# An expert layer by gathered rows, and by dense matmuls over both whole tables

## The chip, the cores and the metric

The kernel runs on one core of one Trainium2 chip. The metric is the device time of a launch in microseconds (us), lower is better; all data are float32. Engines: PE (TensorE, matmuls; PEld its weight loads), DVE (VectorE), ACT (ScalarE), POOL (GpSimd), SP (SyncE, which issues DMAs).

## What is computed

Two transformer blocks on 256 tokens of width 2048. The first mixes four kinds of token mixer and a convolutional FFN of width 5632, the second has a sparse and a sliding-window attention and then a layer of 16384 experts, which is what the change touches:

```python
def peer(xn, wq, subkeys, u, v):
    q = (xt @ wq).reshape(T, PEER_HEADS, 2, PEER_QDIM // 2)
    s1 = jnp.einsum('thd,nd->thn', q[:, :, 0], subkeys[0])
    s2 = jnp.einsum('thd,nd->thn', q[:, :, 1], subkeys[1])
    v1, i1 = lax.top_k(s1, PEER_TOPK)
    v2, i2 = lax.top_k(s2, PEER_TOPK)
    cand = (v1[..., :, None] + v2[..., None, :]).reshape(T, PEER_HEADS, -1)
    sc, ci = lax.top_k(cand, PEER_TOPK)
    idx = e1 * PEER_NKEYS + e2        # e1, e2: i1, i2 at ci // 16, ci % 16
    gate = jax.nn.softmax(sc, axis=-1)
    h = jax.nn.gelu(jnp.einsum('cd,chkd->chk', xc, u[idx]))
    return jnp.einsum('chk,chkd->cd', gate * h, v[idx])
```

There are 8 heads with 16 picks each, so 128 picks a token. An expert's number is a row e1 and a column e2 of a grid of 128 x 128. The tables u and v have 16384 rows of 2048 floats, 134 MB each. After the layer come the residual sum, a last norm and the output.

## The kernel before

Tokens stand in two tiles of 128 (t = 0, 1), one token a partition; `x` holds the residual stream [128, 2, 2048], and `hT` the normed input turned, [128 features, 16, 256 tokens]. Weights are streamed by SP in units of 1 MB through `ring`, four slots of 8 KB a partition: a unit is loaded when the matmuls on the slot's earlier unit have counted `unit_used`, and PE waits on the slot's semaphore. `project` (L789) multiplies on 512 columns, the FFN's up and gate projections (L1041) on 256, its down projection (L1054) on 512 with whole 8 KB rows in the ring.

The expert layer of before follows out2, the second block's output projection:

- `norm(4)`, `norm_turn(3)` (L773) and `norm_cols(3)` (L488) make hT. PE then makes the queries with each token tile by itself (L1189): eight blocks of 128 matmuls on 128 columns, each followed by ACT's copy out of PSUM (L727), which PE waits for. Keys are scored (L1198) and copied by ACT (L730), eight banks in all.
- DVE picks: the best 16 of 128 on 16 sides (`choose_sides`, L1699 to L1706), the best 16 of 256 sums in 8 heads (`choose_sums`), the experts' numbers (`name_experts`, L1739 to L1746), the softmax (`pick_weights`, L1753 to L1759) with ACT's exp (L734) between. For tile 1 this is cut up among the first steps of tile 0.
- POOL copies eight expert numbers (L447) and starts eight indirect DMAs (L456): each brings one row of u for each of 128 tokens, 1 MB, into one of eight row slots (four in `proj`, four in `ring`). Over both tiles and both tables that is 512 gathers.
- DVE takes each gathered row: a product with the token's input summed to one number (L1773, 256 times) for u, and after ACT's gelu of all of them, x += weight * row (L1811, 256 times) for v. Every use returns the slot to POOL by `row_used`.

```python
slot = row_slots[s % ROWS]
link(vec.tensor_tensor_reduce(slot, slot, xs[:, t], 1.0, 0.0, ALU.mult, ALU.add, peer["h16"][:, 0, s:s + 1]), "row_used", wait=(s == 15))
```

The end is L1814 (x is complete), the norm, the scaling by final_norm (L1818) and two stores by SP.

Of the kernel before, what the change touches and what calls it, by code (L numbers as in the profile page):

```python
# [156 lines left out]
def build(nc, a, out, scratch):  # L171
# [120 lines left out]
    choice = [carve(base, {"hot": (PICKS, TOP), "val": (SIDES, TOP), "at_f": (SIDES, TOP), "hi_f": (1, PICKS), "lo_f": (1, PICKS), "e1": (1, PICKS), "e2": (1, PICKS)})
              for base in (flat_proj, arena[:])]
    spare = flat_proj[:, 4 * D:]
    peer |= carve(spare, {"best": (2 * HEADS, TOP), "h": (2, PICKS), "weight": (2, PICKS), "keys": (2, P), "keysT": (2, P), "h16": (1, 16), "total": (1, 2 * HEADS),
                          "at_u": (2 * SIDES, TOP), "pick_u": (2 * HEADS, TOP), "expert": (2, PICKS), "now": (2, 8)})
    row_slots = [flat_proj[:, D * s:D * (s + 1)] for s in range(4)] + [ring[:, s].rearrange("p k n -> p (k n)") for s in range(4)]
# [1550 lines left out]
```

## Time and profile before

| | us |
|---|---|
| median of 3 runs | 3982.63 |
| lowest, highest | 3982.62, 3986.85 |
| span of the profiled execution | 3985.6 |
| PE busy / DVE busy in it | 2187.0 / 1962.2 |
| ACT busy / POOL busy in it | 343.6 / 1297.3 |
| moved by DMA | 932.83 MB |

The page lists the profiled execution by its span, first to last instruction, and gives no other time of it; the three runs' times lie between 3.0 us below that span and 1.3 above it. A line such as L1773 is a line of the kernel; a group shows its name and shapes, how often it ran, its busy time and mean ns, and how long its engine was idle ahead of it and on whom. The clock column is the granted TensorE clock as a share of full speed.

### The profile page before, as it was taken

Reading aid. Unit: us, or ns where it says so; the run is one execution under the profiler, and the core shown is the slowest. Engines: PE = TensorE matmul, PEld = TensorE weight load, DVE = VectorE, ACT = ScalarE, POOL = GpSimd, SP = SyncE. Lnnn points to the kernel's source line nnn. Section 1 sums busy time; section 2 is a strip of 40 time slices with the busy share of each in tenths; the row PEclk is TensorE's granted clock in tenths of the full one; section 3 lists DMA queues with packets and bytes.
Section 4 is the critical chain, followed back from the end, with each engine's and each line's share of the span. In section 5 each row is a group of like instructions: output and inputs, shape, how many; then the busy total and the mean of one; then the engine's idle time right before and its main releaser. Section 6 shows DMA issues by size and latency. Waiting matters only on the chain.

```text
span 3985.6 us, 26773 instructions
## 1 busy us (share of the span) xinstructions
PE 2187.0 (55%) x8774; PEld 1503.0 (38%) x8774; DVE 1962.2 (49%) x2297; ACT 343.6 (9%) x713; POOL 1297.3 (33%) x712
## 2 busy tenths in 40 slices
PE   0899853588999999998898898700000000000000
PEld 0444642545888887443448756700000000000000
DVE  7664165311000000001004511799998888888887
ACT  0000222101011110000103501000000000000000
POOL 2111140000000000000000000177788888888886
PEclk9999875789999999999997999955555555555555
DMA  9898200023444444443640035799899999999998
GB/s 375 333 416 349 67 34 0 1 86 136 157 148 152 153 148 147 157 148 115 203 144 18 0 110 187 282 403 411 341 416 391 374 390 372 374 373 376 378 359 340
DMA packets 236362, 932.83 MB, mean 234 GB/s; under 512 B 20059, under 2 KB 25363, under 8 KB 164115
## 3 DMA queue, kind: packets, MB, share of 16 engines
q0 software_dynamic: 99840, 637.57, 40.1%
q1 hardware_dynamic: 136197, 294.46, 21.7%
q8 instruction: 28, 0.46, 0.0%
q14 instruction: 25, 0.20, 0.0%
q10 hardware_dynamic: 272, 0.13, 0.0%
HBM read 928.91 MB, written 2.15 MB: 234 GB/s over the span
## 4 chain that ended last, share of the span: by engine, by line
PE 50%; DVE 22%; DMA 10%; POOL 8%; issue 6%; ACT 2%; DVEq 0%; SPq 0%; POOLq 0%; ACTq 0%
PE ps L789 16%; PE ps L1041 15%; PE ps L1054 8%; DVE x L1811 6%; POOL ring L456 4%; DVE ring L1773 4%; DVE proj L1773 4%; PE ps L1189 3%; POOL proj L456 3%; DMA ring<-in_w_in 3%; DMA proj<-in_peer_v,proj 2%; DMA ring<-in_peer_u,proj 2%; DMA ring<-in_peer_v,proj 2%; DMA arena<-in_w_mod 1%; DVE arena L1261 1%
## 5 line engine op out<-in xcount | busy, mean ns | idle before, releaser
L447 POOL COPY proj<-proj 128x8 int32 x64 | 109.8, 1716 | 1999.7 <-DVE proj L1746 1957.0
L1041 PE MATMUL ps<-hT,ring 128*128 128x256 f32 x2816 | 608.0, 379 | 1.4 <-ACT hT L488 1.4
L1041 PEld LDWEIGHTS ps<-hT,ring 128*128 128x128 f32 x2816 | 535.0, 190 | 74.3 <-issue 1.7
L789 PE MATMUL ps<-ring,hT 128*128 128x512 f32 (+2 forms) x1216 | 492.8, 567 | 12.1 <-DMA ring<-in_w_in 10.7
L1811 DVE SCALAR_TENSOR_TENSOR x<-proj,x 128x2048 f32<-128x2048 f32 x128 | 301.3, 2354 | 84.2 <-DMA proj<-in_peer_v,proj 73.7
L789 PEld LDWEIGHTS ps<-ring,hT 128*128 128x128 f32 x1216 | 226.1, 197 | 279.0 <-issue 255.4
L1811 DVE SCALAR_TENSOR_TENSOR x<-ring,proj,x 128x2048 f32<-128x2048 f32 x128 | 301.0, 2352 | 30.2 <-DMA ring<-in_peer_v,proj 13.4
L1054 PE MATMUL ps<-ring,arena 128*128 128x512 f32 x704 | 304.1, 595 | 2.7 <-ACT arena L651 2.7
L456 POOL DMA_INDIRECT ring<-in_peer_v,proj x128 | 291.9, 2281 | 39.0 <-issue 39.0
L1773 DVE CUSTOM_DVE_ANT_0 proj<-proj,yT 128x2048 f32<-128x2048 f32 x128 | 288.5, 2289 | 21.4 <-DMA proj<-in_peer_u,proj 18.2
L1773 DVE CUSTOM_DVE_ANT_0 ring<-ring,yT 128x2048 f32<-128x2048 f32 x128 | 289.5, 2292 | 18.6 <-DMA ring<-in_peer_u,proj 17.5
L456 POOL DMA_INDIRECT proj<-in_peer_v,proj x128 | 267.4, 2089 | 58.6 <-issue 29.3
L456 POOL DMA_INDIRECT proj<-in_peer_u,proj x128 | 257.2, 2009 | 57.9 <-issue 29.3
L456 POOL DMA_INDIRECT ring<-in_peer_u,proj x128 | 237.6, 1856 | 40.4 <-issue 38.7
L789 PE MATMUL ps<-ring,yT 128*128 128x512 f32 x512 | 223.0, 598 | 13.6 <-DVE yT L1414 12.6
L1054 PEld LDWEIGHTS ps<-ring,arena 128*128 128x128 f32 x704 | 134.3, 191 | 172.1 <-issue 172.1
L1560 DVE SCALAR_TENSOR_TENSOR arena<-ps,vcols,arena 128x255 f32<-128x255 f32 x44 | 18.2, 476 | 331.0 <-ACT arena L644 331.0
L1261 DVE SCALAR_TENSOR_TENSOR arena<-arena,c_col 128x1024 f32 x120 | 154.2, 1285 | 49.9 <-DMA arena<-in_w_mod 46.8
L397 POOL DMA_DIRECT2D arena<-in_w_mod x96 | 67.8, 706 | 287.3 <-DVE arena L1261 178.7
L1575 DVE TENSOR_TENSOR arena<-ps,gates 128x512 f32<-128x512 f32 x8 | 5.2, 686 | 305.5 <-PE ps L1054 305.4
L789 PEld LDWEIGHTS ps<-ring,yT 128*128 128x128 f32 x512 | 98.2, 192 | 138.5 <-issue 138.5
L1569 DVE TENSOR_TENSOR proj<-arena,ps 128x1024 f32 x11 | 13.4, 1221 | 227.4 <-PE ps L1041 227.4
(379 smaller groups left out, 2250.8 us busy)
## 6 DMA issues: line engine op xcount, KB each, us to landing
arena<-in_w_mod POOLq DMA_DIRECT2D x96, 1024.0 KB
ring<-in_w_in SPq DMA_DIRECT2D x68, 1024.0 KB, 12.8
ring<-in_ffn_w_gate SPq DMA_DIRECT2D x44, 1024.0 KB, 5.1
ring<-in_ffn_w_up SPq DMA_DIRECT2D x44, 1024.0 KB, 5.2
ring<-in_ffn_w_down SPq DMA_DIRECT2D x44, 1024.0 KB, 4.8
ring<-in_w_out SPq DMA_DIRECT2D x32, 1024.0 KB, 5.1
ring<-in_peer_wq SPq DMA_DIRECT2D x32, 1024.0 KB, 5.0
arena<-bias_rows SPq DMA_DIRECT2D x1, 4096.0 KB, 14.4
```

Source lines behind the costliest of these rows:

```text
L397: pool_eng.dma_start(mod["ring"][:, j % 4], w_mod[:, 2 * j:2 * j + 2, cols]).then_inc(sem(f"mod_slot{j % 4}"), 16)
L447: pool_eng.tensor_copy(expert_now[:, half, :], expert[:, t, bass.ds(i * (2 * ROWS) + ROWS * half, ROWS)]).then_inc(sem("experts_now"), 1)
L456: pool_eng.indirect_dma_start(row_slots[s], None, table, bass.IndirectOffsetOnAxis(expert_now[:, half, s:s + 1], 0))\
L789: ins = pe.matmul(ps[:, 2 * (b % 2) + t, 0:w], lhs[:, KS * s + k, P * t:P * (t + 1)], ring[:, s, k, 0:w], start=(s == 0 and k == 0), stop= ...
L1041: ins = pe.matmul(ps[:, 4 * m + f, 0:T], ring[:, s, k, P * f:P * (f + 1)], hT[:, KS * s + k, :], start=(s == 0 and k == 0), stop=(s == SLO ...
L1054: ins = pe.matmul(ps[:, 2 * n + t, :], ffn["act"][:, par, s, P * t:P * (t + 1)], ring[:, s, n, :], start=(start and s == 0), stop=(stop an ...
L1189: ins = pe.matmul(ps[:, f, 0:P], ring[:, s, k, P * f:P * (f + 1)], hT[:, KS * s + k, P * t:P * (t + 1)], start=(s == 0 and k == 0), stop=( ...
L1261: ins = vec.scalar_tensor_tensor(out=to, in0=w, scalar=c, in1=to, op0=ALU.mult, op1=ALU.add)
L1560: ins = vec.scalar_tensor_tensor(out=ffn["gate"][:, f, 1:T], in0=ps[:, f, 0:T - 1], scalar=vcols[:, 1, bass.ds(i * 4 + (44 + f), 1)], in1= ...
L1569: link(vec.tensor_tensor(act_store[:, bass.ds(i * 4, 4), :], ffn["gate"], ps[:, 4:8, 0:T], ALU.mult), "up_free", wait=False)
L1773: link(vec.tensor_tensor_reduce(slot, slot, xs[:, t], 1.0, 0.0, ALU.mult, ALU.add, peer["h16"][:, 0, s:s + 1]), "row_used", wait=(s == 15))
L1811: link(vec.scalar_tensor_tensor(out=x[:, t], in0=row_slots[s % ROWS], scalar=peer["weight"][:, t, bass.ds(i * 16 + s, 1)], in1=x[:, t], op ...
```

## The change

Both tables are read whole, once, in order. Experts with the same column e2 form block b = e2 of 128 experts (partition e1); the host lays u out as [block, feature in a group of 128, group, expert] and v as [block, expert, feature], so that a block is 1 MB and 8 KB a partition in both.

- SBUF: yT, gates, proj and arena become parts of one tensor `big`, whose 128 KB a partition later hold `G` [expert row, block, token].
- Queries for both token tiles together: four blocks of 64 matmuls on 256 columns, in PSUM banks 0 to 3 and 4 to 7 in turn. Scores of both tiles follow, 64 matmuls.
- Hidden layer for every expert: block b is 16 matmuls of 128 x 128 by 256 tokens in bank b % 4, and ACT's gelu of them. For blocks 0 to 39 it goes to G[:, b]; meanwhile DVE picks for both tiles, then exp and softmax.
- The picks (row, column, weight) are turned by PE. For each token, 128 picks by 128 rows one-hot times the weight, and 128 picks by 128 columns one-hot, are made by DVE, four tokens a group; their product on PE is the dense 128 x 128 matrix of weights of that token. In group s (of 64) DVE multiplies the columns of blocks below 40 + s into G, ACT copies the others into G, and block 40 + s is computed in between; `weigh` later multiplies a block's gelu, left in PSUM, into G for the tokens already there.
- Table v: block b is 8 matmuls of G[:, b] by 512 features, all 8 PSUM banks accumulate over 128 blocks, and two DVE operations add them to x.
- Gathers, POOL's part in the layer, L1773 and L1811 are gone. Constants shrink and load in two tables, ffn_norm no longer as rows, final_norm at the end into hT.

```diff
-for _n, _c in (("in1", 12), ("out1", 4), ("up", 22), ("down", 11), ("in2", 7), ("out2", 4), ("wq", 8)):
+for _n, _c in (("in1", 12), ("out1", 4), ("up", 22), ("down", 11), ("in2", 7), ("out2", 4), ("wq", 4), ("u", 32), ("v", 32)):
...
-    yT = sb("yT", [P, KT, T])
+    flat_hT = hT[:].rearrange("p k t -> p (k t)")
+    big = sb("big", [P, P * T])
+    yT = big[:, 0:2 * D].rearrange("p (k t) -> p k t", t=T)
+    gates = big[:, 2 * D:4 * D].rearrange("p (g n) -> p g n", g=2)
+    proj = big[:, 4 * D:4 * D + NT * W1].rearrange("p (t n) -> p t n", t=NT)
+    arena = big[:, 4 * D + NT * W1:4 * D + NT * W1 + 12800]
...
+    G = big[:].rearrange("p (b t) -> p b t", t=T)
+    GROUP = 4
+    GROUPS = T // GROUP
+    FIRST = 40
+    hot = carve(tab[:, TAB_AT["anti"][0]:], {"row": (2, GROUP, P), "col": (2, GROUP, P)})
+    row_of = vrows[:].rearrange("p a b -> p (a b)")[:, 0:T]
+    col_of = vrows[:].rearrange("p a b -> p (a b)")[:, T:2 * T]
+    weight_of = vcols[:].rearrange("p a b -> p (a b)")[:, 0:T]
...
+        stream(w1v["peer_wq_2"], BLK["wq"], 4, 0)
+        load("norm_in", flat_hT[:, 0:D], a["final_norm_2"].partition_broadcast(P))
...
+        for name, table in (("u", a["peer_u_2"]), ("v", a["peer_v_2"])):
+            with sp.Fori(0, P // SLOTS) as i:
+                for s in range(SLOTS):
+                    sp.wait_ge(*at("unit_used", i * SLOTS + (BLK[name] * SLOTS + s - SLOTS + 1)))
+                    sp.dma_start(ring[:, s].rearrange("p k n -> p (k n)").unsqueeze(1), table.rearrange("b p n -> p b n")[:, bass.ds(i * SLOTS + s, 1), :])\
+                      .then_inc(sem(f"slot{s}"), 16)
...
-        for phase, table in enumerate((a["peer_u_2"], a["peer_v_2"])):
-            for t in range(NT):
-                pool_eng.wait_ge(*at("experts", t + 1))
-                base = PICKS * (NT * phase + t)
-                with pool_eng.Fori(0, PICKS // (2 * ROWS)) as i:
-                    for half in range(2):
...
-                        pool_eng.tensor_copy(expert_now[:, half, :], expert[:, t, bass.ds(i * (2 * ROWS) + ROWS * half, ROWS)]).then_inc(sem("experts_now"), 1)
-                        for s in range(ROWS):
...
-                            pool_eng.sem_inc(sem("pool_turn"), 1)
-                            pool_eng.indirect_dma_start(row_slots[s], None, table, bass.IndirectOffsetOnAxis(expert_now[:, half, s:s + 1], 0))\
-                                    .then_inc(sem(f"row{s}"), 16)
...
+        def hidden(b, i, bank):
+            act.wait_ge(*at("unit_used", i + (SLOTS * BLK["u"] + b + 1)))
+            to = G[:, b, :] if isinstance(i, int) else G[:, bass.ds(i + b, 1), :].rearrange("p o t -> p (o t)")
+            act.activation(to, ps[:, bank, 0:T], ACT.Gelu_apprx_tanh).then_inc(sem("hidden"), 1)
...
+        with act.Fori(0, 20, SLOTS) as i:
+            for s in range(SLOTS):
+                hidden(s, i, s)
+        best_exp(0)
+        with act.Fori(20, 36, SLOTS) as i:
+            for s in range(SLOTS):
+                hidden(s, i, s)
+        best_exp(1)
+        for b in range(36, FIRST):
+            hidden(b, 0, b % 4)
+        for s in range(GROUPS):
+            b = FIRST + s
+            n = GROUP * (s + 1)
+            act.wait_ge(*at("unit_used", SLOTS * BLK["u"] + b + 1))
+            if n < T:
+                act.activation(G[:, b, n:T], ps[:, b % 4, n:T], ACT.Gelu_apprx_tanh)
+            act.activation(ps[:, b % 4, 0:n], ps[:, b % 4, 0:n], ACT.Gelu_apprx_tanh).then_inc(sem("hidden"), 1)
+            act.wait_ge(*at("spread_vec", s + 1))
+            act.copy(G[:, b:P, GROUP * s:GROUP * (s + 1)], ps[:, 4 + s % 2, :].rearrange("p (t e) -> p e t", t=GROUP)[:, b:P, :]).then_inc(sem("spread_act"), 1)
+        for b in range(FIRST + GROUPS, P):
+            act.wait_ge(*at("unit_used", SLOTS * BLK["u"] + b + 1))
+            act.activation(ps[:, b % 4, 0:T], ps[:, b % 4, 0:T], ACT.Gelu_apprx_tanh).then_inc(sem("hidden"), 1)
...
+        def wq_block(i, par):
+            for s in range(SLOTS):
+                pe.wait_ge(sem(f"slot{s}"), i * 32 + 16 * (BLK["wq"] + par + 1))
+                for k in range(KS):
+                    for f in range(4):
+                        ins = pe.matmul(ps[:, 4 * par + f, 0:T], ring[:, s, k, P * f:P * (f + 1)], hT[:, KS * s + k, :],
+                                        start=(s == 0 and k == 0), stop=(s == SLOTS - 1 and k == KS - 1))
+                ins.then_inc(sem("unit_used"), 1)
...
+        wq_block(0, 0)
+        pe.wait_ge(*at("keys_out", 1))
+        wq_block(0, 1)
+        for par in range(2):
+            pe.wait_ge(*at("wq_out", par + 1))
+            wq_block(1, par)
+        pe.wait_ge(*at("wq_out", 4))
...
+        def hidden(i, b):
+            s = b % SLOTS
+            pe.wait_ge(sem(f"slot{s}"), i * (16 // SLOTS) + 16 * (BLK["u"] + b // SLOTS + 1))
+            rows = ring[:, s].rearrange("p k n -> p (k n)")
+            for k in range(KT):
+                ins = pe.matmul(ps[:, b % 4, 0:T], rows[:, P * k:P * (k + 1)], hT[:, k, :], start=(k == 0), stop=(k == KT - 1))
+            ins.then_inc(sem("unit_used"), 1)
...
+        for b in range(4):
+            pe.wait_ge(*at("score_out", b + 1))
+            hidden(0, b)
+        with pe.Fori(0, 32, SLOTS) as i:
+            for s in range(SLOTS):
+                pe.wait_ge(*at("hidden", i + (s + 1)))
+                hidden(i, 4 + s)
+        pe.wait_ge(*at("score_out", 8))
+        pe.wait_ge(*at("picked", NT))
+        for m in range(3):
+            for t in range(NT):
+                q = NT * m + t
+                ins = pe.transpose(ps[:, 6 + q // 4, P * (q % 4):P * (q % 4 + 1)], peer["pick"][:, m, t, :], ident)
+        ins.then_inc(sem("picks_turned"), 1)
+        for b in range(36, FIRST):
+            pe.wait_ge(*at("hidden", b - 3))
+            hidden(0, b)
+        for s in range(GROUPS):
+            b = FIRST + s
+            pe.wait_ge(*at("hot", s + 1))
+            if s >= 2:
+                pe.wait_ge(*at("spread_act", s - 1))
+                pe.wait_ge(*at("spread_vec", s - 1))
+            for j in range(GROUP):
+                ins = pe.matmul(ps[:, 4 + s % 2, P * j:P * (j + 1)], hot["row"][:, s % 2, j, :], hot["col"][:, s % 2, j, :],
+                                start=True, stop=True)
+            ins.then_inc(sem("spread"), 1)
+            pe.wait_ge(*at("hidden", b - 3))
+            if s >= 4:
+                pe.wait_ge(*at("weighed", s - 3))
+            hidden(0, b)
+        for b in range(FIRST + GROUPS, P):
+            pe.wait_ge(*at("weighed", b - FIRST - 3))
+            hidden(0, b)
+        pe.wait_ge(*at("weighed", P - FIRST))
+        pe.wait_ge(*at("spread_vec", GROUPS))
+        for b in range(P):
+            s = b % SLOTS
+            pe.wait_ge(*at(f"slot{s}", 16 * (BLK["v"] + b // SLOTS + 1)))
+            for t in range(NT):
+                for n in range(4):
+                    ins = pe.matmul(ps[:, 4 * t + n, :], G[:, b, P * t:P * (t + 1)], ring[:, s, n, :], start=(b == 0), stop=(b == P - 1))
+            ins.then_inc(sem("unit_used"), 1)
...
-        def dot_rows(i, t):
-            for s in range(16):
-                arrived(i, PICKS * t, s)
-                slot = row_slots[s % ROWS]
-                link(vec.tensor_tensor_reduce(slot, slot, xs[:, t], 1.0, 0.0, ALU.mult, ALU.add, peer["h16"][:, 0, s:s + 1]), "row_used", wait=(s == 15))
-            link(vec.tensor_copy(peer["h"][:, t, bass.ds(i * 16, 16)], peer["h16"][:, 0, :]))
...
+            vec.wait_ge(*at("score_out", 4 * t + 4))
+            choose_sides(t, range(SIDES))
+            add_sides(t)
+            choose_sums(t, range(HEADS))
+            shift_best(t)
+            name_experts(t)
+        for t in range(NT):
+            pick_weights(t)
+        vec.wait_ge(*at("picks_turned", 1))
+        vec.tensor_copy(row_of, ps[:, 6, 0:T])
+        vec.tensor_copy(col_of, ps[:, 6, T:2 * T])
+        link(vec.tensor_copy(weight_of, ps[:, 7, 0:T]))
+        def one_hot(s):
+            if s >= 2:
+                vec.wait_ge(*at("spread", s - 1))
+            for j in range(GROUP):
+                t = GROUP * s + j
+                vec.tensor_scalar(hot["row"][:, s % 2, j, :], tb("iota"), row_of[:, t:t + 1], weight_of[:, t:t + 1], ALU.is_equal, ALU.mult)
+            wide = [P, GROUP, P]
+            vec.tensor_tensor(hot["col"][:, s % 2], tb("iota").unsqueeze(1).to_broadcast(wide), col_of[:, GROUP * s:GROUP * (s + 1)].unsqueeze(2).to_broadcast(wide), ALU.is_equal)\
+               .then_inc(sem("hot"), 1)
+        def weigh(b, n):
+            vec.wait_ge(*at("hidden", b + 1))
+            vec.tensor_tensor(G[:, b, 0:n], ps[:, b % 4, 0:n], G[:, b, 0:n], ALU.mult).then_inc(sem("weighed"), 1)
+        one_hot(0)
+        one_hot(1)
+        for s in range(GROUPS):
+            b = FIRST + s
+            vec.wait_ge(*at("spread", s + 1))
+            vec.wait_ge(*at("hidden", b))
+            mine = G[:, 0:b, GROUP * s:GROUP * (s + 1)]
+            vec.tensor_tensor(mine, ps[:, 4 + s % 2, :].rearrange("p (t e) -> p e t", t=GROUP)[:, 0:b, :], mine, ALU.mult).then_inc(sem("spread_vec"), 1)
+            if s + 2 < GROUPS:
+                one_hot(s + 2)
+            vec.wait_ge(*at("spread_act", s + 1))
+            weigh(b, GROUP * (s + 1))
+        for b in range(FIRST + GROUPS, P):
+            weigh(b, T)
+        vec.wait_ge(*at("unit_used", SLOTS * (BLK["v"] + P // SLOTS)))
+        for t in range(NT):
+            rows = x[:, t].rearrange("p (n d) -> p n d", n=4)
+            ins = vec.tensor_tensor(rows, ps[:, 4 * t:4 * t + 4, :], rows, ALU.add)
+        link(ins, "x_done")
...
+    u = arrays["in_peer_u_2"].reshape(P, P, KT, P)
+    arrays["in_peer_u_2"] = np.ascontiguousarray(u.transpose(1, 3, 2, 0)).reshape(P, P, D)
+    arrays["in_peer_v_2"] = np.ascontiguousarray(arrays["in_peer_v_2"].reshape(P, P, D).transpose(1, 0, 2))
+    arrays["in_tab"], arrays["in_tab_bias"] = TAB, TAB_BIAS
```

PE around the picks, of the changed kernel; `big` holds G, the queries and the picks, `tab` the constants and one-hots. L1209 is the hidden layer, L1224 the turning of the picks, L1236 the one-hot products; the loop above (blocks 4 to 35) closes at the branch.

```order
L1209 MATMUL ps<-hT,ring 128x256 [waits slot3,hidden]
L1209 MATMUL ps<-hT,ring 128x256 x15
L1215 REGISTER_ALU
L1215 COMPARE_AND_BRANCH
L1224 MATMUL ps<-tab,big 128x128 [waits picked,score_out]
L1224 MATMUL ps<-tab,big 128x128 x5
L1209 MATMUL ps<-hT,ring 128x256 [waits slot0,hidden]
L1209 MATMUL ps<-hT,ring 128x256 x15
```

PE's matmuls of the hidden layer thus wait once for the picks, between blocks 35 and 36; before, PE had no work behind its last scores.

DVE in the first two groups of the spread phase, of the changed kernel (L1850 multiplies the product into G, L1833 and L1835 make one-hots, L1841 weighs a block).

```order
L1850 TENSOR_TENSOR big<-ps,big 128x40x4 [waits hidden,spread]
L1833 TENSOR_SCALAR tab<-tab,vrows,vcols 128x128 [waits spread]
L1833 TENSOR_SCALAR tab<-tab,vrows,vcols 128x128 x3
L1835 TENSOR_TENSOR tab<-tab,vrows 128x512
L1841 TENSOR_TENSOR big<-ps,big 128x4 [waits hidden,spread_act]
L1850 TENSOR_TENSOR big<-ps,big 128x41x4 [waits hidden,spread]
```

One-hots for the group after next stand between the product of a group and the weighing, which waits for ACT's copy of that same group.

## Rows read from the trace of the kernel before

**Rows 1.** The page: span, TensorE's busy tenths and the DMA's in 40 slices.
```profile
span 3985.6 us, 26773 instructions
PE   0899853588999999998898898700000000000000
DMA  9898200023444444443640035799899999999998
```

**Rows 2.** Stretches: length, busy us (count) of PE, PEld, DVE, ACT, POOL, clock, DMA, GB/s.
```profile
960.00:1568.00 608.00, 607.57 (x2815) 534.88 (x2816) 48.61 (x99) 61.08 (x77) 0.00 (x0) 1.00 0.46 150
1571.00:1875.00 304.00, 303.83 (x704) 134.27 (x704) 0.00 (x0) 10.27 (x10) 0.00 (x0) 0.99 0.39 140
2439.00:2501.00 62.00, 58.70 (x515) 57.82 (x516) 5.20 (x11) 2.34 (x4) 0.00 (x0) 1.00 0.76 254
2573.00:3971.00 1398.00, 0.00 (x0) 0.00 (x0) 1238.98 (x1003) 2.44 (x5) 1156.07 (x567) 0.50 0.96 381
```

**Rows 3.** The page's groups: DVE's work on gathered rows.
```profile
L1773 DVE CUSTOM_DVE_ANT_0 proj<-proj,yT 128x2048 f32<-128x2048 f32 x128 | 288.5, 2289 | 21.4 <-DMA proj<-in_peer_u,proj 18.2
L1773 DVE CUSTOM_DVE_ANT_0 ring<-ring,yT 128x2048 f32<-128x2048 f32 x128 | 289.5, 2292 | 18.6 <-DMA ring<-in_peer_u,proj 17.5
L1811 DVE SCALAR_TENSOR_TENSOR x<-proj,x 128x2048 f32<-128x2048 f32 x128 | 301.3, 2354 | 84.2 <-DMA proj<-in_peer_v,proj 73.7
```

**Rows 4.** Timeline of PE, 2430 to 2505 us: start, length, line, shapes, count.
```profile
2432.56 5.43 PE L773 MATMUL ps<-tab,yT 128*128 128x128 f32 x32 [9.91 <-ACT yT L480]
2439.31 14.55 PE L1189 MATMUL ps<-hT,ring 128*128 128x128 f32 x128
...
2500.82 3.84 PE L1198 MATMUL ps<-proj,arena 128*128 128x128 f32 x32 [0.77 <-ACT arena L727]
```

**Rows 5.** DVE alone from the first top-8 to the shifted scores, tile 0.
```profile
2505.40:2558.90 53.50, 52.64 (x208) 1.00 0.69 236
```

**Rows 6.** Timeline of DVE at the end: x is complete.
```profile
3970.68 0.06 DVE L1814 MEMSET stat<- 128x1 f32 x1 [0.24 <-DVE x L1811]
```

**Rows 7.** One line's instructions, L1041 and L1054: ns min/median/max, first and last start.
```profile
L1041 PE MATMUL ps<-hT,ring x2816: 379/379/478, 960.4 to 1568.1; 128*128 128x256 f32 x188
L1054 PE MATMUL ps<-ring,arena x704: 592/592/1061, 1571.2 to 1874.6; 128*128 128x512 f32 x176
```

**Rows 8.** The same view: lines whose shapes are near the new ones.
```profile
L488 ACT ACTIVATE hT<-ps,vcols x16: 465/470/475, 1903.9 to 2438.0; 128x256 f32<-128x256 f32 x16
L1560 DVE SCALAR_TENSOR_TENSOR arena<-ps,vcols,arena x44: 471/474/484, 992.0 to 1545.7; 128x255 f32<-128x255 f32 x44
L1575 DVE TENSOR_TENSOR arena<-ps,gates x8: 680/686/691, 1875.3 to 1883.6; 128x512 f32<-128x512 f32 x8
L1569 DVE TENSOR_TENSOR proj<-arena,ps x11: 1220/1221/1222, 1016.1 to 1568.6; 128x1024 f32 x11
L1739 DVE TENSOR_SCALAR vrows<-proj x4: 226/226/227, 2542.8 to 2871.6; 128x128 uint32<-128x128 uint32 x4
L1742 DVE TENSOR_TENSOR proj<-proj,tab x2: 2293/2293/2293, 2543.3 to 2550.8; 128x2048 f32<-128x2048 f32 x2
```

**Rows 9.** Timeline of ACT, then DVE, around the exp of tile 0.
```profile
2571.17 1.28 ACT L734 ACT_TABLE_LOAD   x1
2572.47 0.31 ACT L734 ACTIVATE proj<-proj 128x128 f32<-128x128 f32 x1
2572.88 0.29 DVE L1757 TENSOR_REDUCE proj<-proj 128x8 f32<-128x128 f32 x1 [13.96 <-ACT proj L734]
...
2573.43 0.29 DVE L1759 TENSOR_TENSOR proj<-proj 128x128 f32<-128x128 f32 x1
```

**Rows 10.** DMA issues: count, KB each, median us to landing.
```profile
ring<-in_ffn_w_down SPq DMA_DIRECT2D x44, 1024.0 KB, 4.8
ring<-in_peer_wq SPq DMA_DIRECT2D x32, 1024.0 KB, 5.0
```

More of the change, by code:

```diff
@@ L108, in tables @@
         hot[bucket[m], m] = 1
-    cols["bucket"] = hot
     neg = np.zeros((P, 384))
@@ L120, in tables @@
         off += c.shape[1]
-    return at, np.concatenate([np.asarray(c, np.float32) for c in cols.values()], axis=1)
-TAB_AT, TAB = tables()
+    return at, np.concatenate([np.asarray(c, np.float32) for c in cols.values()], axis=1), np.concatenate([hot, neg], axis=1)[0:32].astype(np.float32)
+TAB_AT, TAB, TAB_BIAS = tables()
 STEPS = {
@@ L290, in build @@
     peer = carve(arena[:], {"q": (SIDES, T), "score": (2, SIDES, P), "sum": (2, SIDES // 2, 256)})
[L292 to L297, printed above, removed]
-    ROWS = len(row_slots)
-    at_u, pick_u = peer["at_u"].bitcast(U32), peer["pick_u"].bitcast(U32)
-    part_u = carve(hst["w2"].rearrange("p a b -> p (a b)"), {"x": (1, PICKS)})["x"][:, 0, :].bitcast(U32)
-    expert = peer["expert"].bitcast(I32)
-    expert_now = peer["now"].bitcast(I32)
+    peer |= carve(flat_proj[:, 8248:], {"hot": (PICKS, TOP), "val": (SIDES, TOP), "at_f": (SIDES, TOP), "digit": (1, PICKS)})
+    peer |= carve(flat_proj[:, 5800:8248], {"best": (2 * HEADS, TOP), "total": (1, 2 * HEADS), "keys": (2, P), "keysT": (2, P), "at_u": (2 * SIDES, TOP),
+                                            "pick_u": (2 * HEADS, TOP), "part_u": (1, PICKS), "pick": (3, NT, PICKS)})
+    at_u, pick_u, part_u = peer["at_u"].bitcast(U32), peer["pick_u"].bitcast(U32), peer["part_u"][:, 0, :].bitcast(U32)
+    G = big[:].rearrange("p (b t) -> p b t", t=T)
[6 more added lines that the diff above has]
+    weight_of = vcols[:].rearrange("p a b -> p (a b)")[:, 0:T]
     block = ctx.enter_context(nc.Block())
@@ L1732, in name_experts @@
         def name_experts(t):
-            mine = choice[t]
-            place = halves("at_f", t)
+            place = halves("at_f")
             picks = pick_u[:, HEADS * t:HEADS * (t + 1), :].rearrange("p h k -> p (h k)")
-            hot = mine["hot"].rearrange("p (h k) i -> p h k i", h=HEADS)
-            for s, (op, arg, f, e) in enumerate(((ALU.logical_shift_right, 4, "hi_f", "e1"), (ALU.bitwise_and, 15, "lo_f", "e2"))):
+            by_head = peer["hot"].rearrange("p (h k) i -> p h k i", h=HEADS)
@@ L1743, in name_experts @@
-                link(vec.tensor_tensor(hot, hot, place[:, :, s, :].unsqueeze(2).to_broadcast([P, HEADS, TOP, TOP]), ALU.mult))
-                link(vec.tensor_reduce(mine[e][:, 0, :], mine["hot"], X_AXIS, ALU.add))
-            link(vec.scalar_tensor_tensor(out=mine["e1"][:, 0, :], in0=mine["e1"][:, 0, :], scalar=float(P), in1=mine["e2"][:, 0, :], op0=ALU.mult, op1=ALU.add))
-            link(vec.tensor_copy(expert[:, t, :], mine["e1"][:, 0, :]), "experts")
+                link(vec.tensor_tensor(peer["hot"], digit.unsqueeze(2).to_broadcast(full), tb("iota", TOP).unsqueeze(1).to_broadcast(full), ALU.is_equal))
@@ new lines, in name_experts, with shift_best @@
+                link(vec.tensor_tensor(by_head, by_head, place[:, :, s, :].unsqueeze(2).to_broadcast([P, HEADS, TOP, TOP]), ALU.mult))
+                link(vec.tensor_reduce(peer["pick"][:, s, t, :], peer["hot"], X_AXIS, ALU.add))
+        def shift_best(t):
+            best = peer["best"][:, HEADS * t:HEADS * (t + 1), :]
+            weight = peer["pick"][:, 2, t, :].rearrange("p (h k) -> p h k", h=HEADS)
+            link(vec.tensor_tensor(weight, best, best[:, :, 0:1].to_broadcast([P, HEADS, TOP]), ALU.subtract))
+            link(vec.tensor_copy(best, weight), "best_shift")
```

135 lines of the change are left out of this document (28 added, 107 removed).

## The prediction

> **What bounds the kernel now.** I read the page first. The span is 3985.6 us, and TensorE's row falls to 0 in the last 14 of 40 slices, while the DMA row stands at 8 or 9 [rows 1]. The table by stage gives the same in numbers: from 2573 to 3971 us TensorE runs nothing, DVE is busy 1239 us of 1398 and the DMA engines are busy 96% at 381 GB/s [rows 2]. So the expert layer, 35% of the span, is no matmul work. Each of its 512 steps gathers 128 rows of 8 KB, 1.05 MB, and DVE spends 2.29 us (table u) or 2.35 us (table v) on it [rows 3]. 537 MB at 381 GB/s are 1409 us, DVE needs 1188 us: the gathers end the waits. What DVE waits for there is landing rows: 73.7 us ahead of one half of v's steps, 18.2 and 17.5 us ahead of u's [rows 3]. The stretch just ahead is TensorE's: eight query blocks of 128 matmuls, 14.55 us each, two score passes of 3.84 us [rows 4]. The choice of experts, 53.5 us a tile on DVE, starts at 2505.4 us [rows 5].
>
> **What is replaced.** Everything from the first query matmul at 2439.3 us to x being complete at 3970.7 us, 1531.4 us [rows 4, 6]. What stands ahead keeps its order. The tail from 3970.7 us, norm and output, stays at 15 us [rows 6]. That the constants load as two tables, that final_norm comes in later, and that SP no longer waits for x before streaming w_out_2, I cost at nothing: each lies beside other work by tens of us.
>
> **Matmul prices.** The issue interval decides, not the mean length of overlapping matmuls. Moving 256 columns: 2816 in 607.7 us, 0.2158 us each; 512 columns: 704 in 303.4 us, 0.431 us; both at a granted clock of 1.00 or 0.99, the upper level of 2.4 GHz [rows 2, 7]. Moving 128: 14.55/128 = 0.114 us [rows 4]. All are f32, as the new ones are. The Trainium skill (FP8 and Floating Point Precision, TensorE Precision Notes) says that true FP32 takes four passes through the array. Four times 512 columns at 2.4 GHz would be 0.853 us a matmul, and by that rule every new term would double and the change would lose; the trace's 0.431 us disagrees, and the sum goes by the trace.
>
> **The sum, along TensorE.**
> - Queries: the token tiles go together, 4 blocks of 64 matmuls on 256 columns: 256 x 0.2158 = 55.2 us. Two PSUM halves alternate, so only the last copy is waited for: 0.77 us as now [rows 4], plus 0.5 us since 1024 columns are copied where 512 were; 1.3 us.
> - Scores: 64 matmuls, 2 x 3.84 = 7.7 us [rows 4]. The first copy of scores frees its bank during the second pass.
> - Hidden layer, all 16384 experts: 128 blocks x 16 x 0.2158 = 442.0 us. Gelu on ScalarE, 256 columns of PSUM, costs about 0.47 us (rows of that shape [rows 8]) of each 3.45 us, and TensorE is three blocks behind that wait.
> - The choice on DVE lies beside it. Scores of tile 0 are copied by about 2501; two tiles at 53.5 us end near 2608 us. TensorE asks for the picks after block 35, at 2439.3 + 64.2 + 36 x 3.45 = 2628 us. So DVE has 20 us in hand, and the late one is ScalarE: the second exp stands behind gelu 35. Gelu 0.47, table load 1.28, exp 0.31, DVE's three steps 0.84 us [rows 8, 9], four handoffs of 0.1: TensorE idles 3.3 us.
> - Picks transposed, 6 matmuls: 0.7 us. One-hot products, 64 groups of 4 matmuls on 128 columns: 256 x 0.114 = 29.1 us.
> - Last gelu and last weighing ahead of table v: 1.3 us.
> - Table v: 128 x 8 = 1024 matmuls x 0.431 = 441.3 us.
> - x plus PSUM: 2 operations on 2048 columns, by 1.221 us for 1024 [rows 8]: 4.9 us, with the handoff 5.0.
> - Two short idles may bring a stretch at 1.2 GHz each; between nothing and 5 us each (10 us at half rate), I take 2 together. After 9.91 us of idle the 32 transposes took 5.43 us [rows 4], where 32 x 0.114 are 3.6.
>
> Sum: 55.2 + 1.3 + 7.7 + 442.0 + 3.3 + 0.7 + 29.1 + 1.3 + 441.3 + 5.0 + 2 = 988.9 us in place of 1531.4. New span 3985.6 - 542.5 = 3443.1 us. The page gives no time apart from the span; the median of the runs, 3982.63 us, is 3.0 below it, so I forecast **3440 us**.
>
> **What must stay hidden.**
> DMA: each block is 1.05 MB, asked for every 3.45 us: 305 GB/s. SP reissues a slot when TensorE leaves it; the block is needed three blocks, 10.3 us, later, and such loads land in 4.8 to 5.0 us [rows 10]. At 140 GB/s the down projection, with the same 8 KB rows, keeps the engines busy 39% of the time; the query stretch 76% at 254 GB/s [rows 2]. By those shares full use is 334 to 359 GB/s. It holds, at 85 to 91% of capacity.
> DVE in the spread phase, per group against 3.45 + 0.46 = 3.91 us of TensorE: one PSUM product of 160 to 412 elements, 0.51 us on the mean between rows of 0.474 and 0.686 us; four tensor_scalars 0.226 each; a 512-column one-hot, a quarter of 2.29 us or 0.6; one weighing of 4 to 256 elements, 0.35. That is 2.4 us [rows 5, 8]. ScalarE: two gelus and a copy, 1.4 us. One-hots are made two groups ahead and PSUM has two spread banks, so the chain DVE, ScalarE, DVE inside a group does not reach TensorE.
>
> **The rivals.**
> 1. *The DMA stream does not hold 305 GB/s.* For it: the 254 GB/s of the query stretch is the most that this queue alone has shown, and there TensorE set the pace. Against: the busy shares, and the gathers' 381 GB/s. Priced at 254 GB/s: 134.2 MB are 528 us a table in place of 475 and 441 us, so 53 + 87 = 140 us, 3580 us. At 280 GB/s it is 42 us. Chance 0.14.
> 2. *The spread phase is bound by DVE and ScalarE.* The products are read out of PSUM with a stride of 512 bytes between neighbours, in runs of 4 written at 16 bytes; no row of before has that form. At the contiguous price, the lower bound, nothing happens. DVE has 1.5 us a group free, about 286 elements at 1.1 ns, so per-element cost would have to be some five times higher; at ten times DVE needs 5.2 us, 64 x 1.3 = 83 us: 3523 us. The same result follows if semaphore turns in the chain add 1.3 us. Chance 0.12. The Trainium skill (SBUF — State Buffer, on cachelines) says that PSUM has 8-byte lines and that non-contiguous access slows matmuls significantly; it gives no factor for DVE, and no row here shows one.
> 3. *Slower: the matmuls run at 1.2 GHz.* 930 us of dense f32 matmuls follow on 2400 us of mixed work. If the clock were withheld through the layer, the terms 55.2, 7.7, 442.0, 29.1 and 441.3 double: +975 us, 4415 us. It decides from 56% of these matmuls at half clock (542.5/975). Against: 608 and 304 us of the same work at 1.00 and 0.99 [rows 2]. Chance 0.02.
> 4. *The gather's removal buys nothing, because both tables are read whole.* It reads 268 MB in place of 537. The time would stand still if the two tables took 917 + 542 = 1459 us, at 184 GB/s: 3983 us. The query stretch shows 254 [rows 2]. Chance 0.01, and it is the whole chance of no change.
>
> **How the numbers follow.** Forecast 0.71, its own range 3428 to 3470: down by the clock term and rounding, up by some us at each handoff. The range of 8 in 10 adds the weaker part of rivals 1 and 2: 3425 to 3560. Faster by over 0.2%, about what a measurement of this kernel tells from no change: 0.71 + 0.14 + 0.12 = 0.97. Same 0.01, slower 0.02.
>
> **What would show it.** Right: TensorE busy from 2439 us to the tail, granted clock near 1; 2048 matmuls on 256 columns at 0.216 us in a span of about 475 us, 1024 on 512 columns in 441; TensorE's waits for ring loads near zero; one idle of 3 us after block 35 with ScalarE's exp ahead of it; DMA at some 300 GB/s and 85 to 90%. Rival 1: many idles ended by ring<-in_peer_u or in_peer_v. Rival 2: group period over 3.9 us, matmuls waiting for the one-hots, the copy or the weighing; DVE's strided product over 1 us. Rival 3: PEclk at 5 and matmul intervals of 0.43 and 0.86 us. The forecast is wrong if table v's stretch is not within 3% of 441 us.

## The result, and the profile after

The changed kernel takes **4412.95 us** (median of 4 runs, 4410.91 to 4419.05), the kernel before 3983.47 us in the same comparison (4 runs, 3982.62 to 3986.85). The ratio is 1.108 (95% interval 1.106 to 1.109): slower by a tenth, where 3440 us were forecast. The profiled execution is the longest of the four, 4419.05 us, with a span of 4417.4 us.

The page of the changed kernel, the lines that answer to [rows 1, 3] (in the two groups: out<-in xcount | busy us, mean ns | idle before):

```profile
span 4417.4 us, 37813 instructions
...
PE 4020.1 (91%) x14924; PEld 2727.0 (62%) x14924; DVE 933.4 (21%) x1970; ACT 425.7 (10%) x972; POOL 134.4 (3%) x136
...
PE   0999654789999999979889999999999999999998
...
PEclk9999666799999999989789999999999999999999
DMA  9896100134444444354004444444334444444443
...
L1209 PE MATMUL ps<-hT,ring 128*128 128x256 f32 x4096 | 895.0, 379 | 0.0
L1255 PE MATMUL ps<-ring,big 128*128 128x512 f32 x2048 | 879.2, 592 | 0.9 <-DVE big L1841 0.9
```

Three things are to be seen. The empty end of TensorE's row is gone: the expert layer is now matmul work to the end, as the change says. TensorE's clock is 9 tenths or more through it. The third is the counts. Line 1209 stands in a loop of 128 blocks by 16 matmuls, 2048 as written; the trace has **4096**. Line 1255 is written 1024 times; the trace has **2048**.

The stages of the changed kernel (length, then busy us of TensorE, weight loads, DVE, ScalarE, GpSimd, granted clock, DMA share, GB/s), to be held against [rows 2]:

```profile
2453.00:2564.00 111.00, 110.87 (x514) 97.30 (x514) 0.42 (x1) 3.04 (x3) 0.00 (x0) 1.00 0.43 142
2572.00:3518.00 946.00, 942.66 (x4620) 836.21 (x4618) 260.60 (x881) 86.89 (x271) 0.00 (x0) 1.00 0.42 141
3518.00:4398.00 880.00, 879.18 (x2048) 389.04 (x2048) 0.42 (x1) 0.31 (x1) 0.00 (x0) 1.00 0.44 150
```

Queries, hidden layer, table v. TensorE is busy over 99% of all three, at a granted clock of 1.00, the upper level of 2.4 GHz. The DMA engines move 141 to 150 GB/s, half of the 305 forecast. So nothing is late and nothing is slow; TensorE has about twice the work that was counted. The first and last starts of each group give the interval of one instruction:

```profile
L1185 PE MATMUL ps<-hT,ring x512: 379/379/382, 2453.2 to 2563.5; 128*128 128x256 f32 x171
```
```profile
L1209 PE MATMUL ps<-hT,ring x4096: 379/379/382, 2572.4 to 3517.5; 128*128 128x256 f32 x196
```
```profile
L1255 PE MATMUL ps<-ring,big x2048: 592/592/697, 3518.8 to 4397.4; 128*128 128x512 f32 x187
```

512 in 110.5 us are 0.216 us each and 2048 in 879 us are 0.429 us each. Those are the prices of [rows 7], 0.2158 and 0.431 us. Each price was right per instruction of the trace, and the trace has two of these per matmul that the kernel writes. The listing of the changed program's own instructions, in the section on the change, has 16 MATMULs a block, so the doubling arises behind it; what splits a matmul in two, no run shows.

The small events on TensorE, from its timeline (start, length, group, the idle ahead and what ended it):

```profile
2453.20 110.67 PE L1185 MATMUL ps<-hT,ring 128*128 128x256 f32 x512
2565.18 7.41 PE L1198 MATMUL ps<-big 128*128 128x128 f32 x64 [1.30 <-ACT big L697]
...
2824.47 0.85 PE L1224 MATMUL ps<-tab,big 128*128 128x128 f32 x6 [3.24 <-DVE big L1810]
...
2852.78 1.05 PE L1236 MATMUL ps<-tab 128*128 128x128 f32 x8
2853.67 7.07 PE L1209 MATMUL ps<-hT,ring 128*128 128x256 f32 x32
...
3518.82 11.43 PE L1255 MATMUL ps<-ring,big 128*128 128x512 f32 x26 [0.92 <-DVE big L1841]
```

A group of 4 one-hot products is x8 and a hidden block of 16 matmuls is x32, while the six transposes of line 1224 are x6. Of the f32 forms here, only the transposes are one record for one written.

### The profile page after: what moved, and what is told of

Read it like the earlier page. It is cut to its first block, busy times and chain, and to the rows that moved or that the text cites. A ratio compares the mean times of both kernels' runs of the same rounds, so it can differ in the third digit from the quotient of the medians.

```text
span 4417.4 us, 37813 instructions
## 1 busy us (share of the span) xinstructions
PE 4020.1 (91%) x14924; PEld 2727.0 (62%) x14924; DVE 933.4 (21%) x1970; ACT 425.7 (10%) x972; POOL 134.4 (3%) x136
## 4 chain that ended last, share of the span: by engine, by line
PE 87%; DVE 6%; DMA 4%; ACT 2%; issue 1%; POOL 1%; SPq 0%; DVEq 0%; ACTq 0%; POOLq 0%
PE ps L1209 20%; PE ps L1255 20%; PE ps L787 14%; PE ps L1039 14%; PE ps L1052 7%; PE ps L1185 3%; DMA ring<-in_w_in 2%; PE ps L1236 1%; DMA big<-in_w_mod 1%; DVE big L1316 1%; PE ps L1110 1%; PE ps L1111 1%; PE ps L893 1%; PE ps L1141 1%; PE ps L755 1%
## 5 line engine op out<-in xcount | busy, mean ns | idle before, releaser
L1209 PE MATMUL ps<-hT,ring 128*128 128x256 f32 x4096 | 895.0, 379 | 0.0
L1255 PE MATMUL ps<-ring,big 128*128 128x512 f32 x2048 | 879.2, 592 | 0.9 <-DVE big L1841 0.9
L1209 PEld LDWEIGHTS ps<-hT,ring 128*128 128x128 f32 x4096 | 773.2, 190 | 102.4
L1255 PEld LDWEIGHTS ps<-ring,big 128*128 128x128 f32 x2048 | 389.0, 190 | 490.7 <-issue 489.3
L1039 PE MATMUL ps<-hT,ring 128*128 128x256 f32 x2816 | 608.0, 379 | 1.5 <-ACT hT L458 1.5
L1039 PEld LDWEIGHTS ps<-hT,ring 128*128 128x128 f32 x2816 | 535.0, 190 | 74.4 <-issue 1.7
L1052 PE MATMUL ps<-ring,big 128*128 128x512 f32 x704 | 304.1, 595 | 2.7 <-ACT big L621 2.7
L1316 DVE SCALAR_TENSOR_TENSOR big<-big,c_col 128x1024 f32 x184 | 236.4, 1285 | 83.9 <-DMA big<-in_w_mod 79.5
L1052 PEld LDWEIGHTS ps<-ring,big 128*128 128x128 f32 x704 | 134.3, 191 | 172.1 <-issue 172.1
L787 PE MATMUL ps<-ring,big 128*128 128x512 f32 x512 | 223.0, 598 | 13.6 <-DVE big L1469 12.6
L787 PEld LDWEIGHTS ps<-ring,big 128*128 128x128 f32 x512 | 98.2, 192 | 138.5 <-issue 138.5
L1841 DVE TENSOR_TENSOR big<-ps,big 128x256 f32<-128x256 f32 (+32 forms) x88 | 29.0, 329 | 511.9 <-ACT big L732 356.5
L443 ACT ACTIVATE big<-x 128x2048 f32<-128x2048 f32 x12 | 22.8, 1903 | 957.3 <-DVE x L1861 884.3
L1185 PE MATMUL ps<-hT,ring 128*128 128x256 f32 x512 | 110.7, 379 | 0.0
L1185 PEld LDWEIGHTS ps<-hT,ring 128*128 128x128 f32 x512 | 97.2, 190 | 13.2
L755 PE MATMUL ps<-tab,big 128*128 128x1 f32 x128 | 27.4, 351 | 85.0 <-DVE big L1316 85.0
L755 PEld LDWEIGHTS ps<-tab,big 128*128 128x128 f32 x128 | 27.6, 333 | 86.4 <-issue 86.2
L387 POOL DMA_DIRECT2D big<-in_w_mod x96 | 68.9, 717 | 284.3 <-DVE big L1316 279.3
```

What stands on the lines that cost most here:

```text
L387: pool_eng.dma_start(mod["ring"][:, j % 4], w_mod[:, 2 * j:2 * j + 2, cols]).then_inc(sem(f"mod_slot{j % 4}"), 16)
L755: ins = pe.matmul(ps[:, bank, j:j + 1], mod["acc"].rearrange("p a b -> p (a b)")[:, P * j:P * (j + 1)], ones[:, 0:1], start=True, stop=True)
L787: ins = pe.matmul(ps[:, 2 * (b % 2) + t, 0:w], lhs[:, KS * s + k, P * t:P * (t + 1)], ring[:, s, k, 0:w], start=(s == 0 and k == 0), stop= ...
L1039: ins = pe.matmul(ps[:, 4 * m + f, 0:T], ring[:, s, k, P * f:P * (f + 1)], hT[:, KS * s + k, :], start=(s == 0 and k == 0), stop=(s == SLO ...
L1052: ins = pe.matmul(ps[:, 2 * n + t, :], ffn["act"][:, par, s, P * t:P * (t + 1)], ring[:, s, n, :], start=(start and s == 0), stop=(stop an ...
L1185: ins = pe.matmul(ps[:, 4 * par + f, 0:T], ring[:, s, k, P * f:P * (f + 1)], hT[:, KS * s + k, :], start=(s == 0 and k == 0), stop=(s == S ...
```

## The experiments

The theory (A) is the count: every f32 matmul that is not a transpose runs as two instructions, 0.43 us per written one on 256 columns and 0.86 on 512. Its main rival (B) is the table stream, the first rival of the prediction: the doubled matmuls might hide a queue that could not have held 305 GB/s either. Times below are medians, each with its ratio to the kernel before and a 95% interval. The comparisons ran at different times and not all on one chip, and the kernel before had medians from 3983.47 to 3997.13 us in them. A difference between times of two comparisons can therefore be off by some 14 us, and where it matters the stretch in the trace is given beside it.

**Half of the hidden matmuls.**

```diff
-            for k in range(KT):
+            for k in range(KT // 2):
...
```

> Leaves out 8 of the 16 matmuls of each block of the hidden layer (half of the features), nothing else: loads, gelu, picks and table v stay. Theory A (TensorE bounds both tables, and each f32 matmul that the kernel writes is two matmul instructions, 0.2158 us each on 256 columns): 128 x 8 x 2 x 0.2158 = 442 us less than the changed kernel, 3971 us; each block then takes 3.45 us and asks the stream for 305 GB/s. Theory B (the stream of 1 MB loads gives no more than the 254 GB/s that this queue had shown in the query stretch of before): 53 us of it are not won, about 4024 us, with waits of TensorE for ring<-in_peer_u.

Measured: 3972.42 us, ratio 0.9946 (0.9921 to 0.9970). That is 440.5 us less than the changed kernel for 1024 written matmuls, 0.430 us each; A gave 3971. In the traces the hidden layer's stretch falls from 945.1 to 504.8 us, by 440.3. The stream brings the 128 blocks of 1.05 MB in the 504.8 us from the first to the last start, 266 GB/s, so it doesn't stop at 254 GB/s, by which the saving would have been smaller and the time 4024 us.

**Half of table v's matmuls.**

```diff
-            for t in range(NT):
+            for t in (b % 2,):
...
```

> Leaves out half of the matmuls on table v: block b is multiplied for token tile b % 2 alone, 4 matmuls in place of 8; all loads stay. Theory A: 128 x 4 x 2 x 0.4293 = 440 us less, 3973 us. Theory B (stream at 254 GB/s): 87 us of it are not won, about 4060 us, with waits for ring<-in_peer_v.

Measured: 3971.22 us, ratio 0.9946 (0.9921 to 0.9971); A gave 3973. 441.7 us for 512 written matmuls are 0.863 us each. In the traces table v's stretch falls from 878.6 to 439.2 us, by 439.4, which is 0.858 us each.

**Both halves: the load that the prediction had in mind.** Both edits together. The two big products then have as many instructions in the trace as the forecast counted.

> Both cuts at once: the expert layer has exactly the number of matmul instructions in the hidden layer and on table v that the forecast counted. Theory A: 4413 - 442 - 440 = 3531 us, which is the forecast of 3440 plus the parts whose instructions were miscounted too (queries 55, one-hot products 29) and some us. Theory B: 3670 us. If the spread phase is bound by DVE and ScalarE once a group leaves TensorE only 4.4 us, the hidden layer stays longer than 475 + 29 us and its groups wait for hot, spread_vec, spread_act or weighed.

Measured: 3532.97 us, ratio 0.8836 (0.8806 to 0.8866); A gave 3531. Its two table stages, with the columns above, and TensorE's timeline in the spread phase:

```profile
2566.00:3071.00 505.00, 501.76 (x2568) 448.02 (x2567) 260.24 (x879) 86.50 (x269) 0.00 (x0) 1.00 0.77 264
3072.00:3511.00 439.00, 438.91 (x1023) 194.48 (x1024) 0.04 (x1) 0.00 (x0) 0.00 (x0) 1.00 0.88 301
```
```profile
2797.77 3.62 PE L1209 MATMUL ps<-hT,ring 128*128 128x256 f32 x16
2801.22 1.05 PE L1236 MATMUL ps<-tab 128*128 128x128 f32 x8
2802.12 3.62 PE L1209 MATMUL ps<-hT,ring 128*128 128x256 f32 x16
```

The two cuts together save 880.0 us, where one by one they save 440.5 and 441.7. Table v takes 439 us at 301 GB/s with TensorE busy throughout, so rival 1 falls: the stream holds the forecast rate. The spread phase has a period of 4.35 us a group (2797.77 to 2802.12): one half block of 3.45 us and eight instructions of 0.11, and TensorE doesn't idle. That is slower than the 3.91 us a group of the forecast, because the one-hot products are doubled here too, so this run alone doesn't try rival 2 at the forecast pace. The next one does.

**A quarter: what the stream can give.**

```diff
-            for k in range(KT):
+            for k in range(KT // 4):
...
-            for t in range(NT):
-                for n in range(4):
+            for t in (b % 2,):
+                for n in (b // 2 % 2, b // 2 % 2 + 2):
...
```

> A quarter of the matmuls of both tables is left (4 of 16 a block in the hidden layer, 2 of 8 on table v); all loads stay. TensorE alone would need 1.73 us a block: 3090 us in all. If the stream ends the waits at the capacity read from the busy shares (334 to 359 GB/s, 2.9 to 3.1 us a block), each table takes 374 to 402 us: about 3340 to 3400 us. If the stream's real ceiling is 254 GB/s (theory B): 4.13 us a block, 528 us a table, about 3640 us.

Measured: 3244.49 us, ratio 0.8123 (0.8098 to 0.8149), faster than expected. The two stages, and the waits of table v's (us in total, times, longest):

```profile
2558.00:2900.00 342.00, 294.67 (x1544) 249.36 (x1542) 260.24 (x879) 86.73 (x270) 0.00 (x0) 0.98 0.95 386
2900.00:3220.00 320.00, 253.92 (x512) 86.70 (x512) 0.51 (x2) 0.02 (x1) 0.00 (x0) 1.00 1.01 418
```
```profile
PEld ps L1255 <- DMA ring<-in_peer_v: 170.6, 127, 2.4
PE ps L1255 <- DMA ring<-in_peer_v: 65.4, 126, 1.6
```

Now every block of table v is waited for, and the limit shows: 418 GB/s, 2.5 us a block, 320 us for the table. The hidden layer takes 342 us; 16.9 of them are one idle at the picks. My estimate of 334 to 359 GB/s, from busy shares, was too low. The share grows in proportion to the rate only at first: 0.44 at 150 GB/s and 0.88 at 301, but 0.95 at 386 and 1.01 at 418.

The same run settles rival 2. Two groups of its spread phase:

```profile
2701.84 1.05 PE L1236 MATMUL ps<-tab 128*128 128x128 f32 x8
2702.73 1.89 PE L1209 MATMUL ps<-hT,ring 128*128 128x256 f32 x8
2704.46 1.05 PE L1236 MATMUL ps<-tab 128*128 128x128 f32 x8
```

A group starts every 2.62 us, well under the forecast's 3.91. TensorE is busy for all 166.00 us from 2673 to 2839 us, the whole phase, so it never waits for the one-hots, the copy or the weighing. The chain through DVE and ScalarE keeps up with more than the pace that the forecast set.

**One instruction for one matmul: the tables in bfloat16.** The loads go to GpSimd's queue and turn f32 into bfloat16 on the way into the ring; the normed tokens and the gelu outputs are held in bfloat16 too. Every written matmul is kept; the two big products take operands rounded to bfloat16.

```diff
+    hTb = big[:, 0:2048].bitcast(BF16).rearrange("p (k t) -> p k t", t=T)
+    half = [ring[:, s].rearrange("p k n -> p (k n)")[:, 0:D // 2].bitcast(BF16) for s in range(SLOTS)]
...
+                    pool_eng.dma_start(half[s].unsqueeze(1), table.rearrange("b p n -> p b n")[:, bass.ds(i * SLOTS + s, 1), :])\
...
-            rows = ring[:, s].rearrange("p k n -> p (k n)")
+            rows = half[s]
...
```

> All matmuls of both tables are there, on bfloat16 operands: POOL's queue loads each block and the DMA casts it to bfloat16 in the ring, hT is copied once to bfloat16 by POOL during the queries, G is bfloat16. Results are rounded to bfloat16 there; queries, scores, picks and one-hot products stay float32. Theory A (what costs is the number of matmul instructions at 0.108 us for 128 columns' worth of clock, not the layer's dense form): each written matmul becomes one instruction without the two-instruction, half-rate form of f32, 0.108 us on 256 columns, TensorE needs 1.73 us a block in both tables, as in e4_quarter, and the time is e4_quarter's 3245 us if the casting loads run as fast as its plain ones, up to 3400 us if they run at 334 GB/s. Theory C (the time per block of the dense form does not depend on the operands' type): 4413 us. A casting stream at half the rate (210 GB/s, 5 us a block) would give 3880 us.

Measured: 3255.62 us, ratio 0.815 (0.813 to 0.817); A gave 3245 for a casting stream as fast as the plain one. The page's two groups, and one place of the timeline:

```profile
L1264 PE MATMUL ps<-ring,big 128*128 128x512 bf16 x1024 | 244.5, 382 | 78.6 <-DMA ring<-in_peer_v 77.7
L1217 PE MATMUL ps<-big,ring 128*128 128x256 bf16 x2048 | 246.5, 275 | 36.5 <-DMA ring<-in_peer_u 26.7
```
```profile
2662.52 1.51 PE L1233 MATMUL ps<-tab,big 128*128 128x128 f32 x6 [16.59 <-DVE big L1819]
```

The same loops now leave 2048 and 1024 instructions, one for each written. This is the plainest evidence for A: the two products keep their loops and sizes, their operands change type, and the count halves (the loads' queue changes too, but it brings no matmul). A block of 16 takes 1.91 us from its first start to its last end:

```profile
2701.49 1.06 PE L1245 MATMUL ps<-tab 128*128 128x128 f32 x8
2702.39 1.91 PE L1217 MATMUL ps<-big,ring 128*128 128x256 bf16 x16
```

With the 0.27 us of one instruction taken off, that is 0.109 us for each of the other 15, a quarter of the 0.43 us of f32: half the instructions, each at half the interval. TensorE waits for the ring in both groups. For table v the stream is the bound, at 322 us (2906.5 to 3228.3). The 16.59 us replace the 3.24 of the changed kernel, as the 16.9 of the quarter run did. TensorE now reaches the picks sooner than DVE finishes choosing: the cover that "The sum" counted at 20 us is used up.

**Table v alone in bfloat16.** The same edit, for v only.

> Table v alone goes through bfloat16 (cast by the DMA, G in bfloat16); the hidden layer stays as in the changed kernel, float32 on SP's queue. Theory A (terms add, each by its instructions or by its stream): table v's stretch falls from 880 us to the 322 us of e5_bf16, 4413 - 558 = 3855 us, and the hidden layer keeps its 945 us. Rival: the two halves of the layer are not independent (G in bfloat16 or the stream's start at the turn from u to v costs something): over 3900 us.

Measured: 3853.24 us, ratio 0.9672 (0.9651 to 0.9693), against 3855 by A.

```profile
L1220 PE MATMUL ps<-hT,ring x4096: 379/379/382, 2570.6 to 3515.7; 128*128 128x256 f32 x196
```
```profile
L1266 PE MATMUL ps<-ring,big x1024: 379/379/390, 3517.0 to 3832.1; 128*128 128x512 bf16 x171
```

The f32 half still has two instructions per written matmul and takes its 945 us, the bfloat16 half has one and takes 315. The two tables' costs add up: nothing is left over from mixing the types.

**The picks later.** The bfloat16 kernel again, with the picks asked for after block 43 in place of 35.

```diff
-    FIRST = 40
+    FIRST = 48
...
-        with act.Fori(20, 36, SLOTS) as i:
+        with act.Fori(20, 44, SLOTS) as i:
...
```

> e5_bf16 with the picks asked for after block 43 in place of 35, and the spread phase begun at block 48 in place of 40. In e5_bf16 TensorE stood idle 16.6 us there, because DVE's two tiles of picks take longer than 36 blocks at 2.5 us. Theory A: eight more blocks of 2.5 us cover it, the hidden layer's stretch of 348 us loses 10 to 16 us, 3256 becomes 3240 to 3246 us. Rival: the gap only moves (DVE is slowed or the four ring slots let the stream run on during the gap anyway): no difference over 3 us.

Measured: 3239.65 us, ratio 0.8134 (0.8113 to 0.8154). The idle ahead of line 1233 falls from 16.59 us to this (engine waited for, us, times):

```profile
  DVE big L1819: 3.2, 1
```

The hidden stretch shrinks from 348 us (2557.3 to 2905.3) to 330 (2567.7 to 2897.5). The medians differ by 16.0 us, but they come from different chips, on which the kernel before differs by 13.3 us; the ratios, 0.815 and 0.8134, have intervals that overlap. What the run shows is the stretch, shorter by 18 us, and the idle, shorter by 13.4. In the profiled executions the layer began 10.4 us later in this version, so the span fell by 8.7 us only (3248.0 to 3239.3). This version is faster than both the kernel before and the changed one, at the price of rounding the operands of two products. Gathers of rounded rows were not tried, so this is no comparison of the two forms at equal precision.

## Why the prediction was wrong

**The step that failed is "Matmul prices", in its count.** I divided 607.7 us by the 2816 instructions of the up projection and 303.4 us by the 704 of the down projection [rows 7], and multiplied by the matmuls that the new code *writes*. The up projection writes 11 x 2 x 4 x 16 = 1408 and the down projection 352. Had I held the counts of [rows 7] against the loops, the price per written matmul would have been 0.43 and 0.86 us. The query matmuls showed it too: eight blocks of 64 written matmuls stand in [rows 4] as x128. The number that I used in "What bounds the kernel now", "eight query blocks of 128 matmuls", is this same mistake. It stands in the section on the kernel before as well, and the changed kernel's "64 matmuls" of scores are 32 written ones.

**The rule that the prediction set aside was right.** The Trainium skill (FP8 and Floating Point Precision, TensorE Precision Notes) gives true FP32 four passes through the array; the estimate from it, four times 512 columns at 2.4 GHz, is 0.853 us. The trace agrees: 879.2 us for 1024 written matmuls are 0.859 us each. The bfloat16 run agrees too, at a quarter of the f32 price. My "the trace's 0.431 us disagrees" compared a whole matmul with half of one.

**The terms**, forecast and measured, from the first query matmul to x complete:

| term | forecast us | measured us | from |
|---|---|---|---|
| queries, with the wait behind | 56.5 | 112.0 | 2453.2 to 2565.2 |
| scores | 7.7 | 7.3 | 2565.2 to 2572.4 |
| hidden, picks, one-hots, bubble | 475.1 | 945.5 | 2572.4 to 3517.9 |
| turn to table v | 1.3 | 0.9 | its idle ahead of L1255 |
| table v | 441.3 | 879.2 | 3518.8 to 4398.1 |
| x plus PSUM | 5.0 | 4.5 | 4398.1 to 4402.6 |
| clock | 2 | 0 | granted 1.00 in all stages |
| sum | 988.9 | 1949.4 | |

The 945.5 us are 4096 x 0.2158 = 884, 64 groups of eight one-hot instructions at 0.89 = 57 (29.1 forecast), the bubble and the transposes. The excess is 960.5 us. With 13.9 us by which the first query began later than before (2453.2 against 2439.3), 3443.1 + 960.5 + 13.9 = 4417.5, the span measured.

**What held.** The bubble at the picks, 3.24 us against 3.3, and the wait behind the queries, 1.30 against 1.3. That the stream and DVE stay off the path at the forecast pace: the run with both halves shows it for the stream, the quarter run for DVE and ScalarE. The tail at 15 us (14.8 measured). And the score passes: their price is that of a whole pass in [rows 4], and the 64 instructions that I called matmuls are the 32 written ones, seen twice; no count of the code came into it. Beside the six transposes it is the one matmul term that came out.

**The rivals.** 1 and 2 didn't occur, and fell even where TensorE was made fast enough to meet them. The third gave 4415 us, almost the time measured, and was still wrong: the clock was 1.00, and the intervals 0.216 and 0.429 us. Twice as many instructions and half the clock give the same time, and only the count and the granted clock tell them apart. The rival that was missing is "the counts of rows 7 don't match the loops", which the trace of before already decided.

**What the kernel would have needed.** Counted in whole, the f32 matmuls of the dense layer cost more than the gathers that they replace (1949.4 us from the first query on, against 1531.4); in bfloat16 the layer falls to about the stream's own time, 320 to 330 us a table, and the idea pays (3239.65 us).

**The 13.9 us at the start.** They come in at one stage, the second block's attention. Where it begins, with a product of 30 columns (line 1089 before, 1087 after), the two kernels are level: 2126.55 and 2126.33 us. From there to the first query matmul it takes 312.8 us before and 326.9 after. The stage in both, with the columns of [rows 2], before first:

```profile
2126.00:2330.00 204.00, 177.03 (x1119) 152.11 (x1120) 105.87 (x389) 89.86 (x354) 0.00 (x0) 0.94 0.03 9
2126.00:2330.00 204.00, 178.06 (x1089) 158.75 (x1090) 105.97 (x388) 89.83 (x354) 0.00 (x0) 0.86 0.00 1
```

DVE and ScalarE do the same work; TensorE's granted clock is lower, 0.86 against 0.94, and it gets fewer matmuls done. Other runs with the new code follow this: 316.5 us at 0.93 (the quarter run), 325.5 at 0.88 (both halves), 326.7 at 0.87 (half of the hidden matmuls). The change leaves that stage's matmuls as they are, and what lowers the clock there in some of the runs stays open.

## What to carry to other kernels

Before a mean or an interval from a trace is multiplied by matmuls of a new loop, hold the trace's count against the count that the old loop writes: in every kernel here an f32 matmul is two instructions in the trace, so its price is twice the interval, 0.43 us on 256 columns and 0.86 on 512. Where a documented rule and a trace differ by a clean factor of two, look for the unit first. And halving a gather's bytes is not enough: the f32 work that replaced it here was longer than the gather, and the dense form paid only in bfloat16, where a matmul costs a quarter.
